# A first weight chunk in two halves, the residual stream's load later, and the closing norm's factor ahead of the root

## The reference, cut to what matters

```
def rmsnorm(x, g):
    y = x * rsqrt(mean(x * x, axis=-1) + EPS)
    return y * g

h = x
h = h + retention_layer(rmsnorm(h, ret_norm), ret_w_in, ret_w_out)
k, v = shared_kv(h, kv_norm, w_kv)
h = h + swa_sink_layer(rmsnorm(h, swa_norm), swa_w_in, sinks, swa_w_out, k, v)
return rmsnorm(h, final_norm)
```

## Time and profile before

| what | value |
|---|---|
| time, median of 3 runs | 2503.83 us (2503.79 to 2503.93) |
| the profiled execution's own time | 2503.58 us |
| its span, first to last instruction | 2501.6 us |
| TensorE busy (matmuls) | 2459.1 us, 98% of the span |
| VectorE, ScalarE, POOL busy | 1151.9, 573.1, 135.5 us |
| bytes moved by DMA | 462.41 MB, 185 GB/s on average |
| first 62.5 us (first slice of 40): DMA | 8 tenths busy, 358 GB/s |

### The profile page before, as it was taken

The page is one execution under the profiler, slowest core; times in us unless marked ns, Lnnn a source line. Parts: engine busy times, 40 slices in busy tenths (PEclk is TensorE's granted clock), DMA queues, the critical chain, the costliest instruction groups (busy, mean ns, idle before and its releaser), DMA issues.

```text
span 2501.6 us, 29504 instructions
## 1 busy us (share of the span) xinstructions
PE 2459.1 (98%) x11600; PEld 2039.5 (82%) x11600; DVE 1151.9 (46%) x1967; ACT 573.1 (23%) x1314; POOL 135.5 (5%) x145
## 2 busy tenths in 40 slices
PE   7999999999999999999999999999999999999998
PEld 6888888877888888888888888888788888888877
DVE  6454554588434233336742423333764233333384
ACT  2221311233211121223421102112442121212142
POOL 2111112211000000000000000000000000000000
PEclk9999999999999999999999999999999999999999
DMA  8766665645644434343554343534255434344423
GB/s 358 271 237 267 241 255 210 252 160 225 232 172 164 168 134 181 125 170 113 208 220 181 135 172 132 199 134 169 92 230 219 159 146 181 134 183 153 168 98 147
DMA packets 43834, 462.41 MB, mean 185 GB/s; under 512 B 4832, under 2 KB 5472, under 8 KB 14560
## 3 DMA queue, kind: packets, MB, share of 16 engines
q1 hardware_dynamic: 34864, 425.07, 45.4%
q10 hardware_dynamic: 8880, 36.18, 3.9%
HBM read 358.47 MB, written 102.76 MB: 184 GB/s over the span
## 4 chain that ended last, share of the span: by engine, by line
PE 91%; DVE 6%; issue 1%; ACT 1%; DMA 0%; POOL 0%; DVEq 0%; SPq 0%; ACTq 0%; POOLq 0%
PE ps L455 29%; PE ps L457 29%; PE ps L456 29%; DVE fr L1029 1%; PE ps L583 1%; PE ps L709 1%; DVE ff L1305 1%; DVE mx L1345 1%; PE ps L719 1%; PE ps L520 1%; DVE ff L1376 0%; DVE whl L1074 0%; DMA raw<-in_stream 0%; ACT ff L980 0%; DVE xlo L1029 0%
## 5 line engine op out<-in xcount | busy, mean ns | idle before, releaser
L455 PE MATMUL ps<-whl,xhi 128*128 128x512 f32 (+1 forms) x1408 | 542.1, 385 | 0.8 <-DVE xlo L1029 0.5
L457 PE MATMUL ps<-whl,xlo 128*128 128x512 f32 (+1 forms) x1408 | 536.1, 381 | 0.0
L456 PE MATMUL ps<-whl,xhi 128*128 128x512 f32 (+1 forms) x1408 | 534.7, 380 | 0.0
L455 PE MATMUL ps<-xhi,whl 128*128 128x512 f32 x768 | 304.3, 396 | 16.6 <-DVE xlo L1033 16.2
L457 PEld LDWEIGHTS ps<-whl,xlo 128*128 128x128 f32 x1408 | 264.7, 188 | 51.5
L455 PE MATMUL ps<-whl,fr 128*128 128x512 f32 x768 | 306.0, 398 | 0.0
L455 PEld LDWEIGHTS ps<-whl,xhi 128*128 128x128 f32 x1408 | 265.0, 188 | 49.0 <-issue 0.9
L456 PEld LDWEIGHTS ps<-whl,xhi 128*128 128x128 f32 x1408 | 265.1, 188 | 48.1
L457 PE MATMUL ps<-whl,fr 128*128 128x512 f32 x768 | 301.4, 392 | 0.0
L457 PE MATMUL ps<-xhi,whl 128*128 128x512 f32 x768 | 300.0, 391 | 0.0
L456 PE MATMUL ps<-xlo,whl 128*128 128x512 f32 x768 | 299.7, 390 | 0.0
(11 more groups left out here) (134 smaller groups left out, 2641.1 us busy)
## 6 DMA issues: line engine op xcount, KB each, us to landing
whl<-split_w SPq DMA_DIRECT2D x132, 2048.0 KB, 7.8
split_w<-whl SPq DMA_DIRECT2D x44, 2048.0 KB, 7.3
raw<-in_stream SPq DMA_DIRECT2D x44, 1024.0 KB, 9.4
ff<-in_x_t ACTq DMA_DIRECT2D x8, 1024.0 KB, 10.1
hres<-in_x ACTq DMA_DIRECT2D x4, 2048.0 KB, 8.7
out<-hres ACTq DMA_DIRECT2D x16, 512.0 KB, 5.0
ff<-in_x ACTq DMA_DIRECT2D x3, 2048.0 KB, 15.1
whl<-split_w SPq DMA_DIRECT2D x6, 1024.0 KB, 6.5
```

The lines of the kernel that those rows point to most:

```text
L455: pe.matmul(dst, lhs[0], rhs[0], start=start, stop=False)
L456: pe.matmul(dst, lhs[0], rhs[1], start=False, stop=False)
L457: return pe.matmul(dst, lhs[1], rhs[0], start=False, stop=stop)
```

## The change

Three things. The load of chunk 0 is made as two DMAs, columns 1024 to 2047 first (`LEAD = 1024`), and POOL and VectorE round and split it half by half with semaphores of their own; TensorE starts when the first half is split and waits for the other ahead of the fifth k tile. The load of x to `hres` is issued behind ACT's first four `xhi` instructions and behind the rope tables. In the last block, VectorE multiplies `hres` by the final gain (`gained`) once the tile has been squared, and by the root (`scaled`) in an instruction of its own, one tile later.

```diff
@@ SP, start
+                if n == 0:
+                    sp.dma_start(raw[0][:, LEAD:CHUNK], stream[0:P, LEAD:CHUNK]).then_inc(lead_loaded.sem, 16)
+                    sp.dma_start(raw[0][:, 0:LEAD], stream[0:P, 0:LEAD]).then_inc(w_loaded[0].sem, 16)
+                else:
+                    sp.dma_start(raw[n % 2][:, 0:width(n)], raw_source(n)).then_inc(w_loaded[n % 2].sem, 16)
@@ POOL, start
-            round_chunk(0)
+            pool.wait_ge(lead_loaded.sem, 16)
+            pool.tensor_scalar(whi[0][:, LEAD:CHUNK], raw[0][:, LEAD:CHUNK], 1.0, 1.0, ALU.mult, ALU.mult).then_inc(lead_hi.sem, 1)
+            pool.wait_ge(w_loaded[0].sem, 16)
+            pool.tensor_scalar(whi[0][:, 0:LEAD], raw[0][:, 0:LEAD], 1.0, 1.0, ALU.mult, ALU.mult).then_inc(w_hi.sem, 1)
@@ TensorE, one_head
-                        w_wait(at, c)
+                        if begin and c == 0:
+                            pe.wait_ge(lead_ready.sem, 1)
+                        else:
+                            w_wait(at, c)
                         for n, k in enumerate(X_ORDER):
                             if c == 0:
+                                if begin and n == 4:
+                                    w_wait(at, c)
@@ ACT, start
-            load_x(0)
             load_ropes(0)
             act.wait_ge(gain_loaded.sem, 16)
             next_hi(Place("start"), 1)
+            load_x(0)
             next_hi(Place("start"), 0)
@@ VectorE, start
-            split_chunk(0)
-            for n in range(KT):
+            dve.wait_ge(lead_hi.sem, 1)
+            dve.tensor_tensor(wlo[0][:, LEAD:CHUNK], raw[0][:, LEAD:CHUNK], whi[0][:, LEAD:CHUNK].bitcast(F32), ALU.subtract).then_inc(lead_ready.sem, 1)
+            for n in range(4):
+                next_lo(at, 0, n)
+            dve.wait_ge(w_hi.sem, 1)
+            dve.wait_ge(lead_ready.sem, 1)
+            dve.tensor_tensor(wlo[0][:, 0:LEAD], raw[0][:, 0:LEAD], whi[0][:, 0:LEAD].bitcast(F32), ALU.subtract).then_inc(w_ready[0].sem, 16)
+            for n in range(4, KT):
                 next_lo(at, 0, n)
@@ VectorE, end of the last block
-                    add_to_h2(1, 0)
-                    add_to_h2(1, 1)
-                    mean_square_of(0)
-                    add_to_h2(1, 2)
-                    mean_square_of(1)
+                    def gained(t):
+                        dve.wait_ge(h2_add.sem, at(h2_add, 5 + t))
+                        dve.wait_ge(sq_sum.sem, at(sq_sum, 5 + t))
+                        dve.tensor_tensor(hres[:, t, :], hres[:, t, :], fn[:, :], ALU.mult).then_inc(h_gained.sem, 1)
+
+                    def scaled(t):
+                        dve.wait_ge(rstd_done.sem, at(rstd_done, 2 + t))
+                        dve.wait_ge(h_gained.sem, t + 1)
+                        dve.tensor_scalar(hres[:, t, :], hres[:, t, :], rstd[:, t:t + 1], None, ALU.mult).then_inc(fin.sem, 1)
+
                     dve.wait_ge(fn_loaded.sem, at(fn_loaded, 1))
-                    norm_tile(b, 0, 2)
-                    add_to_h2(1, 3)
-                    mean_square_of(2)
-                    norm_tile(b, 1, 3)
-                    mean_square_of(3)
-                    norm_tile(b, 2, 4)
-                    norm_tile(b, 3, 5)
+                    for t in range(TT):
+                        add_to_h2(1, t)
+                        if t:
+                            scaled(t - 1)
+                        mean_square_of(t)
+                        gained(t)
+                    scaled(3)
```

More of the change, by code:

```diff
@@ L55 @@
 CHUNK = 2048
+LEAD = CHUNK // 2
 HEAD_CHUNKS = 8
@@ L193, in build @@
         w_ready = [count(f"w_ready{i}", head=4, post=7, unit=16) for i in range(2)]
+        lead_loaded = count("w_lead_loaded")
+        lead_hi = count("w_lead_hi")
+        lead_ready = count("w_lead_ready")
         w_stored = [count(f"w_stored{i}", head=4, post=7, unit=16) for i in range(2)]
@@ L300, in build @@
         fin = count("final_normed", post=4)
+        h_gained = count("final_gained")
         nprev_set = count("nprev_set", post=1, credit=1)
@@ L350, in _ @@
                     sp.wait_ge(w_ready[n % 2].sem, 16 * (n // 2))
-                sp.dma_start(raw[n % 2][:, 0:width(n)], raw_source(n)).then_inc(w_loaded[n % 2].sem, 16)
+                if n == 0:
[3 more added lines that the diff above has]
+                    sp.dma_start(raw[n % 2][:, 0:width(n)], raw_source(n)).then_inc(w_loaded[n % 2].sem, 16)
                 if n == 0:
```

## The result

The changed kernel took 2512.47 us (median of 11 runs, 2509.62 to 2514.89), the kernel before on the same chip 2503.95 (11 runs, 2503.45 to 2509.24): ratio 1.003, interval [1.0021, 1.0038]. It is slower by 8.5 us, outside the predicted range. The profiled execution took 2512.47, span 2510.5, so **8.9 us** more than the one before. These 8.9 are what has to be found.

What follows compares the result with a forecast made beforehand. The prediction took TensorE and its weight loads, 91% of what ended last, as the bound. It added +0.9 (late diagonal), +1.7 (clock) and +1.1 (end), +3.7 us on 2503.58, for 2507.3 us, range 2502.3 to 2509.6.

Steps and rivals of the forecast that it cites:

- Half chunk: Start: first matmul at 13.0, 3.2 us earlier; second half hidden; chunk 0 over at 25.4.
- The 12.36 us: Start: TensorE's working time on chunk 0 in the kernel before, added to 13.0 to end chunk 0 at 25.4.
- x late: Start: x, issued later, lands at 21.2 instead of 17.05, so xms comes at 25.5.
- The failed step: Start: diagonal ready at 29.4 against 26.63; TensorE goes on at 29.45 instead of 28.57, +0.9 us (+0.4 to +1.4).
- The clock: Start: TensorE's 4.1 us idle drops the granted clock to half rate, +1.7 us (0 if it stays up).
- Block 0: Wait at 578.57 shifts with the start; rival: it goes away (2502) or another arises (2511 or so), chance 0.12.
- The end: Last block: the multiplication by the gain delays the adds, the last by 1.1; +1.1 us in all (+0.3 to +2.2).
- The stores decide: End: four 512 KB stores, 5.2 us, first issued behind the last square, which slips 1.1, set the end.
- the one on the other side (x not late): Rival, start: x lands at 19.0, TensorE goes on at 26.7, clock stays up: 2502.8 us; chance 0.18.

Runs made afterwards that it cites:

- the filled wait: The changed kernel with 24 unused matmuls ahead of the start's small ones, keeping TensorE busy through most of its wait: 2510.57 us, ratio 1.0023.
- The halved chunk: The changed kernel with x loaded at its old place and the old end, leaving only the first chunk in two halves: 2503.58 us, ratio 0.9996.
- the matmuls put ahead: Halved first chunk alone, small matmuls inside chunk 1, start reordered, plus 11 unused matmuls ahead of the first real one: 2502.99 us, ratio 0.9989.

## Why the prediction was wrong

- **Half chunk.** Right: first matmul forecast 13.0, seen 13.3; second half hidden. Chunk 0 was over at 26.2 (its last matmul's start and 0.23) instead of 25.4: 0.3 from the first matmul, and 0.5 because nine matmuls ran 0.43 us apart ahead of the full clock, where before it were six. That number is no property of the kernel: three executions whose start is that of the kernel before had six, seven and fourteen, 0.2 us each. The 12.36 us that the forecast carried over came from the one with the fewest.
- **x late.** Right in kind and nearly in size: 21.2 forecast, 21.73 seen; xms 25.5 and 26.03. Between 12 and 16 us the queues moved 428 and 425 packets, so turn by turn held.
- **The failed step** is "I take 28.35 for its end ..., plus 1.0 for the copy, vcol and diagonal: ready at 29.4" and the +0.9 from it, bounded at +1.4. It measured **+3.55**: x 0.5 later; the root not at 28.35 but at 29.30 (x's 0.5 is in that), because the split held it until 28.40 and it then took another 0.90, nearly its whole 1.03, where I had counted 0.45; and `vcol` 1.74 instead of 0.18, because it began 0.17 after POOL's next rounding and ended with it (29.46 + 1.90 and 29.63 + 1.74). The last I had not looked for at all. I had asked whether VectorE holds POOL, from the one row where it did, and not whether POOL holds VectorE. The start with the root ahead of the split shows both delays gone together and 3.4 us back. Of the 5.2 us by which the forecast fell short, this step is 2.65, the clock's size 1.06, and block 0's clock 1.6; the stretches left out take 0.1 back.
  The Trainium skill (SBUF — State Buffer, SBUF: two separate sides) says just this of VectorE instructions with two SBUF inputs or in a two-port mode: one pair of ports is shared with POOL, whichever engine's instruction starts first has it for its whole length, and the other stands still. The trace agrees in both directions, 3.01 against 1.03 for the root and 1.74 against 0.18 for `vcol`. What I had weighed, the Trainium skill's GPSIMD Engine Reference (Specifications), names the shared interfaces and not who wins.
- **The clock.** The mechanism was right (shown by the filled wait), the size was not: +1.7 forecast, **+2.76** measured. I took over the 3.4 us at half rate that stood behind a 3.7-us wait; here the clock was low for 6.8 us (31.0 to 37.8), of which 1.1 passed in the wait. Why the low stretch is twice as long is not shown: in two of the other executions the same 3.67-us wait had one of 6.8 us as well, each time with the fall 1.5 us ahead of the wait's end.
- **Block 0.** I wrote of its waits that "what stands there follows TensorE's own steps and shifts with it". The waits did (1.98 and 3.68 us in all kernels), the clock did not: **+1.6** at a wait where it had stayed up before. It fell there in 7 of the 13 profiled executions, in those with the early x and those with the late one. All seven are among the nine kernels with the halved chunk, and none of the four without it; with one execution each, that is a hint and no proof. So this term is no sure part of the change; it fits the executions' spread (2509.6 to 2514.9), and a single trace can't price it.
- **The end.** The number came out, +1.1 forecast and measured, and the hold of the adds was right: the last add's slip 1.1 forecast and 1.5 seen (0.28 of it an idle time ahead of the first `gained` that the kernel with only the new end doesn't have), 1.23 for `gained`, 0.75 for `scaled` (0.69 taken), 1.47 for the root (held). The path was wrong: "The stores decide" did not hold. In both kernels the last store is issued 0.03 us behind the last tile's instruction (2498.45 before, 2507.28 here) and lands 2.8 us later, with the queue not in its way. It is the last tile that sets the end, ready 1.0 later than before relative to the first add, where 0.7 was forecast; the 0.28 made up the rest, which was luck. The Trainium skill (VectorE: DVE Perf Modes, Mode 2x_2P) gives the fp32 tensor_scalar two elements per cycle and the tensor_tensor one; 0.75 against 1.23 agrees.
- **Of the rivals** the one on the other side (x not late) describes what happens when the line is moved back. It came to 2503.4 in the profiled execution and 2503.9 in the median, instead of the 2502.8 worked out. The small matmuls start at 27.32, not 26.7: the diagonal is ready at 27.2, not 26.6.

What stays open: why the clock falls at a wait of 1.98 us in some executions only, whether the halved first chunk makes that fall more likely, and where the 0.7 us behind block 0 go. The halved chunk is 1.0 us ahead at 480 us and does not show in the median; the spread that the clock makes, up to 1.5 us at the start and 1.6 in block 0, is larger than that.

## What to carry over

A transfer that is "needed later" has its need at the end of a chain: count what stands behind its landing on each engine, with the other engines' queues running against it. Where a small VectorE or POOL instruction on the critical chain comes to lie beside a long one of the other, price it with the rest of the long one's time, in both directions. A gain at the head of a kernel bounded by TensorE is real only if the next waits shrink as well, and a wait that grows can be paid again through the clock (2.76 us for the 5.77-us wait here, nothing for waits of 1.34 and 0.98).

## What the runs showed of the hardware

- POOL and VectorE hold each other from whichever side starts first: VectorE's `vcol` 1.74 (alone 0.17), a 4-column copy 1.77 (0.16), and a 4-column tensor_scalar 1.81 beside POOL's rounding in the kernel with only the new end; POOL's root 3.01 to 3.18 (alone 1.03) and its rounding 2.98 (alone 1.91) beside VectorE's split.
- At half clock the 512-column matmuls start 0.43 us apart, at full clock 0.23. The number at half rate at the start varied from 6 to 14 between executions, without the matmuls put ahead. Around the 5.77-us wait the clock read 0.50 for 6.8 us, at block 0's wait of 3.66 to 3.71 us for 3.4 in eleven executions and for 6.8 in two.
- The same 1.98-us wait at the same place was followed by a fall of the clock in 7 of 13 profiled executions; each of those lost 1.6 us. At the 2.58-us wait it fell in 11 of 13, at the cost of 0.1 to 0.4 us.
